# Layer 0 of a hybrid encoder: feature-major inputs from the host, and 1/rms applied behind the projections

## What is computed

```
h  = rms_norm(x, mix_norm_g)                 # x * rsqrt(mean(x^2) + eps) * g
proj = h @ w_in                              # 1024 x 4184 columns: mLSTM q,k,v,o and gates;
                                             # neighbourhood attention q,k,v; GLA q,k,v,g and a
x += mixer(proj) @ w_out                     # three kinds of heads, both directions
x += cross_attention(rms_norm(x, xattn_norm_g), rms_norm(mem, mem_norm_g))
x += (gelu(conv3(a)) * g) @ w_down           # a, g = rms_norm(x, ffn_norm_g) @ w_up
```

## Time and profile before

| | |
|---|---|
| median of 3 runs | 880.57 us (878.48 to 882.46) |
| time of the profiled execution | 878.24 us |
| its span, first to last instruction | 876.3 us |
| around the span | 1.9 us |
| TensorE busy | 861.8 us, 98% |
| VectorE busy | 596.0 us, 68% |
| ScalarE busy | 496.1 us, 57% |
| DMA | 146.78 MB, mean 168 GB/s |

### The profile page before, as it was taken

The page is one execution under the profiler, slowest core; times in us unless marked ns, Lnnn a source line. Parts: engine busy times, 40 slices in busy tenths (PEclk is TensorE's granted clock), DMA queues, the critical chain, the costliest instruction groups (busy, mean ns, idle before and its releaser), DMA issues.

```text
span 876.3 us, 14948 instructions
## 1 busy us (share of the span) xinstructions
PE 861.8 (98%) x6338; PEld 798.1 (91%) x6338; DVE 596.0 (68%) x820; ACT 496.1 (57%) x689; POOL 14.3 (2%) x35
## 2 busy tenths in 40 slices
PE   8999999999999999999999999999999899999997
PEld 8999998889889999999999999988898899999996
DVE  6887678757657666666577885887665666656655
ACT  7954663658647445445567546745755645445444
POOL 5000000000000000000000000000000000000000
PEclk9999999999999999999999999999999999999999
DMA  9735452364255555555448254335435365555541
GB/s 329 201 102 177 156 178 103 112 226 144 97 193 190 195 190 195 192 191 194 145 140 257 72 171 165 127 115 192 135 109 191 127 212 190 193 196 190 192 169 48
DMA packets 114665, 146.78 MB, mean 168 GB/s; under 512 B 10600, under 2 KB 94760, under 8 KB 114600
## 3 DMA queue, kind: packets, MB, share of 16 engines
q1 hardware_dynamic: 114456, 145.57, 49.7%
q10 hardware_dynamic: 144, 0.26, 0.1%
HBM read 144.77 MB, written 1.05 MB: 166 GB/s over the span
## 4 chain that ended last, share of the span: by engine, by line
PE 92%; ACT 3%; DVE 3%; issue 1%; DMA 0%; ACTq 0%; DVEq 0%
PE bank L665 26%; PE bank L666 25%; PE bank L667 25%; PE bank L706 4%; PE bank L743 2%; PE bank L832 2%; DVE wlo L1455 2%; PE bank L1017 2%; ACT whi L1096 1%; ACT yhi L1119 1%; PE bank L872 1%; PE bank L762 1%; PE bank L849 1%; DVE ylo L1710 1%; PE bank L882 1%
## 5 line engine op out<-in xcount | busy, mean ns | idle before, releaser
L1455 DVE TENSOR_TENSOR wlo<-raw,whi 128x2048 fp32r<-128x2048 f32 (+3 forms) x144 | 306.2, 2133 | 106.1 <-ACT whi L1096 105.2
L1096 ACT ACTIVATE whi<-raw 128x2048 fp32r<-128x2048 f32 (+3 forms) x144 | 257.4, 1793 | 53.5 <-PE bank L667 48.4
L665 PE MATMUL bank<-yhi,whi 128*128 128x256 f32 x704 | 195.1, 277 | 0.5 <-DVE ylo L1471 0.5
L666 PE MATMUL bank<-ylo,whi 128*128 128x256 f32 x704 | 194.6, 276 | 0.0
L667 PE MATMUL bank<-yhi,wlo 128*128 128x256 f32 x704 | 194.6, 276 | 0.0
L665 PEld LDWEIGHTS bank<-yhi,whi 128*128 128x128 f32 x704 | 132.2, 188 | 1.6 <-issue 0.7
L666 PEld LDWEIGHTS bank<-ylo,whi 128*128 128x128 f32 x704 | 132.2, 188 | 0.8
L667 PEld LDWEIGHTS bank<-yhi,wlo 128*128 128x128 f32 x704 | 132.2, 188 | 0.0
L665 PE MATMUL bank<-xhi,whi 128*128 128x256 f32 x320 | 91.4, 286 | 2.2 <-DVE wlo L1455 1.2
L665 PE MATMUL bank<-whi,xhi 128*128 128x512 f32 (+2 forms) x256 | 90.1, 352 | 0.0
L667 PE MATMUL bank<-xhi,wlo 128*128 128x256 f32 x320 | 88.9, 278 | 0.0
(11 more groups left out here) (268 smaller groups left out, 1373.1 us busy)
## 6 DMA issues: line engine op xcount, KB each, us to landing
raw<-in_w_up SPq DMA_DIRECT2D x44, 1024.0 KB, 5.0
raw<-in_w_down SPq DMA_DIRECT2D x22, 1024.0 KB, 4.8
raw<-in_w_in SPq DMA_DIRECT2D x10, 1024.0 KB, 7.3
raw<-in_w_xk SPq DMA_DIRECT2D x8, 1024.0 KB, 5.1
raw<-in_w_xv SPq DMA_DIRECT2D x8, 1024.0 KB, 4.9
raw<-in_w_out SPq DMA_DIRECT2D x8, 1024.0 KB, 4.8
raw<-in_w_xq SPq DMA_DIRECT2D x8, 1024.0 KB, 5.7
raw<-in_w_xo SPq DMA_DIRECT2D x8, 1024.0 KB, 4.9
```

The lines of the kernel that those rows point to most:

```text
L665: mm(o, s_hi, m_hi, start=first, stop=False, skip_group_check=True)
L666: mm(o, s_hi, m_lo, start=False, stop=False, skip_group_check=True)
L1096: A(weight(whi, gu), raw[:, gu % RING, 0:SIZE[gu]], ACT.Copy).then_inc(hi_done, 1)
L1455: tt(weight(wlo, gu), raw[:, gu % RING, 0:SIZE[gu]], weight(whi, gu), ALU.subtract).then_inc(lo_done, 1)
```

## The change

All of it is in layer 0, and the other layer keeps its code.

- The host passes x and mem a second time, laid out by features (`x_turned`, `mem_turned`, 1 MB each). The token-major x and mem are still loaded, x because it is the residual and gives the squares.
- xhi and xlo are made from the loaded blocks with the gain only. The two `normed`, the 16 transposes of x and the wait for x before gq go. gq, mix and qk0 are loaded and split in halves. nqk4 comes ahead of qk0. `keep_clock` runs 6 matmuls instead of 12.
- x itself is loaded after qk1. The squares follow the high part of qk1 on ScalarE; VectorE makes 1/rms as a column (`r1`, and half of it) and TensorE spreads it into a row on all partitions (`rx`, two matmuls in the midst of qk0), copied to `xr`.
- Feature-major results (mix, gq, nqk4, qk0 to qk2, nq, nk, gk) are multiplied by `xr` on VectorE. gq, nqk4, nq, nk and gk were emptied by ScalarE before. Token-major results (v, nv, gv, o, gg) get 1/rms as the scale of the ScalarE instruction that empties them already.
- mem: the squares are on ScalarE behind `conv(0)`, the row `rm` takes the place of the 16 transposes, and one VectorE instruction scales `memT` (128x2048) in head 3.
- GpSimd starts its constants at once, the parameter columns come in three DMAs, and half of qk1 is ahead of gp.

The diff, cut to its core:

```diff
+    if l:
+        fm("qk0", "w_in", (0, 256))
     fm("nqk4", "w_few", (2 * P, P))
+    if l == 0:
+        fm("qk0", "w_in", (0, 256))
     fm("qk1", "w_in", (256, 256))
...
+HALVED = ("gq", "mix", "qk0")
...
+        xr = carve(T)
...
+            def turned_rows(i):
+                sp.dma_start(xT[:, 2 * i:2 * i + 2, :], a["x_turned"][:, 2 * i:2 * i + 2, :]).then_inc(turned_in[i], 16)
             def load(gu):
                 if gu >= RING:
                     sp.wait_ge(lo_done, gu - RING + 1)
                 (l, _), m, k0, nk, cols = UNITS[gu]
                 dst = raw[:, gu % RING, 0:SIZE[gu]].rearrange("p (k n) -> p k n", k=nk)
+                if l == 0 and UNITS[gu][0][1] in HALVED:
+                    i = HALVED.index(UNITS[gu][0][1])
+                    c, n = cols[0]
+                    src = a[m][l, c // P] if m == "w_few" else a[m][l, :, c:c + n].rearrange("(k p) n -> p k n", p=P)
+                    sp.dma_start(dst[:, 0:4], src[:, 0:4]).then_inc(half_in[i], 16)
+                    if i == 0:
+                        turned_rows(0)
+                    sp.dma_start(dst[:, 4:KT], src[:, 4:KT]).then_inc(landed[gu % RING], 16)
+                    return
...
+                    for i in range(1, KT // 2):
+                        turned_rows(i)
+                if name == "qk2" and l == 0:
+                    for t in range(TT):
+                        sp.dma_start(h[:, t, :], a["x"][t * P:(t + 1) * P, :]).then_inc(tok_in[t], 16)
+                    sp.dma_start(pcols[:, 0, KT:], a["params"][:, 0, KT:]).then_inc(prm_in[0], 16)
                     sp.wait_ge(const_ready, 3)
                     load_gates(0)
+                if name == "va" and l == 0:
                     for t in range(TT):
                         sp.dma_start(mtm[:, t, :], a["mem"][t * P:(t + 1) * P, :]).then_inc(mem_in, 16)
+                if name == "vb" and l == 0:
+                    sp.dma_start(pcols[:, 1, :], a["params"][:, 1, :]).then_inc(prm_in[1], 16)
+                    sp.dma_start(memT[:], a["mem_turned"]).then_inc(mem_turned_in, 16)
...
-            pool.wait_ge(xn_ready, TT)
-            for v, x in ((gq, 0.0), (gk, 0.0), (perm, 0.0), (mlm, 0.0), (glm, 1.0), (bdm, 1.0), (win, 3e38),
-                         (ones, 1.0), (reset, 1.0), (mv, 1.0)):
+            for v, x in ((gq, 0.0), (gk, 0.0), (perm, 0.0), (ones, 1.0), (mv, 1.0)):
                 step(g.memset(v[:], x))
...
-            keep_clock(12, ps[BANK[0, "qk0"]])
+            keep_clock(6, ps[BANK[0, "qk0"]])
...
+                    fm_unit("nqk4", "n1")
+                else:
+                    fm_unit("nqk4", "n1")
+                    fm_blocks("qk0", "n1", [(0, 0, KT), (1, 0, 4)])
+                    pe.wait_ge(root_in, 1)
+                    free("rx")
+                    for t in range(TT):
+                        last = mm(bank("rx")[:, t * P:(t + 1) * P], r1[:, t, 0:1].broadcast_to([P, P]), ident[:], start=True, stop=True)
+                    last.then_inc(te_done, 1)
+                    fm_blocks("qk0", "n1", [(1, 4, KT)])
+                    fm_blocks("qk1", "n1", [(0, 0, 4)])
+                pe.wait_ge(const_ready, 4)
                 free("gp")
                 is_drained(pe, l, "mix")
                 mm(bank("gp")[0:64, 0:T], perm[:, 0, :], gsb[:, :], start=True, stop=True)
                 mm(bank("gp")[0:64, T:2 * T], perm[:, 1, :], gsb[:, :], start=True, stop=True).then_inc(te_done, 1)
-                if l:
-                    fm_blocks("qk1", "n1", [(0, 0, 4)])
+                fm_blocks("qk1", "n1", [(0, 0, 4) if l else (0, 4, KT)])
...
-                    pe.wait_ge(memn_ready, TT)
-                    for i in range(4):
-                        free(f"mt_{i}")
-                        for kk in range(2):
-                            for t in range(TT):
-                                k = 2 * i + kk
-                                last = nc.tensor.transpose(bank(f"mt_{i}", 2, T)[:, kk, t * P:(t + 1) * P],
-                                                           mtm[:, t, k * P:(k + 1) * P], ident[:])
-                        last.then_inc(te_done, 1)
+                    pe.wait_ge(mem_root_in, 1)
+                    free("rm")
+                    for t in range(TT):
+                        last = mm(bank("rm")[:, t * P:(t + 1) * P], rmem[:, t:t + 1].broadcast_to([P, P]), ident[:], start=True, stop=True)
+                    last.then_inc(te_done, 1)
...
+                def token_scale(t, half=0):
+                    return 0.5 ** half if l else r1[:, t, half:half + 1]
                 def take(nm):
+                    if l == 0 and nm in SCALED:
+                        return
...
+                def input_hi(ks):
+                    for k in ks:
+                        if k % 2 == 0:
+                            act.wait_ge(turned_in[k // 2], 16)
+                        A(xhi[:, k, :], xT[:, k, :], ACT.Copy, scale=pcol[:, R_MIX + k:R_MIX + k + 1]).then_inc(xhi_ready, 1)
                 if l == 0:
-                    act.wait_ge(prm_in, 16)
+                    hi_half("gq", 0)
+                    act.wait_ge(gain_in, 16)
+                    input_hi(range(2))
+                    hi_half("gq", 1)
+                    input_hi(range(2, KT))
+                    hi_half("mix", 0)
+                    hi_half("mix", 1)
+                    split_hi("nqk4")
+                    hi_half("qk0", 0)
+                    hi_half("qk0", 1)
+                    split_hi("qk1")
+                    for t in range(TT):
+                        act.wait_ge(tok_in[t], 16)
+                        square_all(h, t)
...
+                    act.wait_ge(prm_in[0], 16)
+                    act.wait_ge(const_ready, 4)
+                    act.wait_ge(mix_scaled, 1)
+                    b = mix_part
                 A(gsb[:, :], b[0:24, 0:T], ACT.Identity, bias=gbias[:, :])
                 A(gaT[96:128, :], b[96:128, 0:T], ACT.Copy)
                 A(gq[0:32, 1, :], b[32:64, 0:T], ACT.Copy, scale=32 ** -0.5)
                 drain(A(gk[0:32, 1, :], b[64:96, 0:T], ACT.Copy))
-                split_hi("qk1")
+                split_hi("qk1" if l else "qk2")
                 conv(0)
...
+                    act.wait_ge(mem_in, 16 * TT)
+                    for t in range(TT):
+                        square_all(mtm, t)
+                act.wait_ge(const_ready, 4)
...
+                    is_filled(act, l, "rm")
+                    drain(A(mr, bank("rm")[:, 0:T], ACT.Copy))
...
+                def input_lo(ks):
+                    for k in ks:
+                        hi_is(dve, l, "n1", k)
+                        stt(xlo[:, k, :], xT[:, k, :], pcol[:, R_MIX + k:R_MIX + k + 1], xhi[:, k, :], ALU.mult, ALU.subtract
+                            ).then_inc(xlo_ready, 1)
+                def xr_for(n):
+                    return xr.rearrange("p (o n) -> p o n", o=1).broadcast_to([P, n, T])
+                def scaled_qk(i):
+                    is_filled(dve, l, f"qk{i}")
+                    tt(qe[:, 2 * i:2 * i + 2, :], bank(f"qk{i}", 2, T), xr_for(2), ALU.mult).then_inc(scaled_ready, 1)
                 if l == 0:
+                    lo_half("gq", 0)
+                    input_lo(range(2))
+                    lo_half("gq", 1)
+                    input_lo(range(2, KT))
+                    lo_half("mix", 0)
+                    lo_half("mix", 1)
+                    split_lo("nqk4")
+                    lo_half("qk0", 0)
+                    lo_half("qk0", 1)
+                    split_lo("qk1")
                     for t in range(TT):
-                        dve.wait_ge(tok_in[t], 16)
-                        normed(t)
-                    dve.wait_ge(prm_in, 16)
-                    split_lo("gq")
-                turned("n1", R_MIX)
-                split_lo("nqk4")
-                if l == 0:
-                    dve.wait_ge(mem_in, 16 * TT)
-                    for t in range(TT):
-                        inverse_root(t)
-                        ts(mtm[:, t, :], mtm[:, t, :], rt[:, t:t + 1], None, ALU.mult).then_inc(memn_ready, 1)
-                split_lo("qk1")
+                        root_ready(t)
+                        link(V.reciprocal(r1[:, t, 0:1], rt[:, t:t + 1]))
+                    ts(r1[:, :, 1], r1[:, :, 0], 0.5, None, ALU.mult).then_inc(root_in, 1)
+                    is_filled(dve, l, "rx")
+                    drain(V.tensor_copy(xr, bank("rx")[:, 0:T]))
+                    is_drained(dve, l, "rx")
+                    is_filled(dve, l, "mix")
+                    tt(mix_part, bank("mix")[:, 0:T], xr, ALU.mult).then_inc(mix_scaled, 1)
+                    dve.wait_ge(const_ready, 4)
+                    is_filled(dve, l, "gq")
+                    drain(stt(gq[:, 0, :], bank("gq")[:, 0:T], 32 ** -0.5, xr, ALU.mult, ALU.mult))
+                    is_filled(dve, l, "nqk4")
+                    b = bank("nqk4")
```

(63 more changed lines are left out.)

138 lines of the change are left out of this document (86 added, 52 removed).

## The result

The changed kernel takes 887.9 us (median of 4 runs, 887.42 to 888.54) against 879.64 us (4 runs, 878.48 to 882.46) in the same session: ratio 1.0091, 95% interval 1.007 to 1.0111. It is slower by some 8 us; the prediction had said 881.7 with a range up to 886.0. The profiled execution took 888.38 us with a span of 886.4; the one of before took 878.24.

A forecast was written before the change was run, and what follows sets the result against it. VectorE was taken to bound nearly as much as TensorE at nq: of 5.5 us head start, waits of 4.85 left 0.6; heads cost 1.7, so +1.1 on 880.57 gave 881.7 us, range 876.0 to 886.0.

The forecast's parts named there:

- Everything behind is the same work with TensorE as its bound and keeps this shift.: After the heads of layer 0: all later work was to keep the shift of +1.1 us unchanged.
- the waits before the first head and nq: TensorE was to wait 2.95 us for `qk_ready` before the score product and 1.15 us for nq's low part.
- head start: TensorE's possible lead from an earlier mix and dropped memory transposes, less the added matmuls: 5.5 us if nothing else were late.
- The paragraph on the clock: At the start: with 12 warming passes the warming ends at 4.4 us, so gq may start at the lower clock.
- rival 4: The lower clock holds through gq into nqk4; 48 passes cost 5.6 us, 4.5 of it absorbed: 882.8 us, chance 0.10.
- qk1 at 14.85 (14.3 and 0.55): ScalarE takes qk1 at 14.85 us: DMA flow reaches its end at 14.3, plus 0.55 for the signal.
- root_in at 20.0: 1/rms of x ready for TensorE at 20.0 us, after squares, roots and reciprocals; TensorE waits 0.75 us.
- rival 3: Slower because x lands late: at 300 GB/s x comes 4.6 us later, giving 886.3 us; chance 0.16.
- With 1.4 us more (nq, nk): Head 2: VectorE's added nq and nk scaling delays the weights to 69.9 us, so TensorE waits 0.7.
- A wait of 1.0: Head 4: gv's second half has its low part at 85.5 us, wanted at 84.4; TensorE waits 1.0.
- Mix starts at 9.45.: Mix's first pass on TensorE was to start at 9.45 us instead of 14.10, a gain of 4.65 us.
- the slack of 0.4 us: In the kernel before, VectorE ends nq's low part at 51.01 us and TensorE starts nq at 51.42.

The follow-up runs named there:

- run 2: The changed kernel with dummy identity matmuls where TensorE waits: 13 before the first score product, 5 before nq, 7 before nv; 885.75 us, ratio 1.0065.
- run 12: The changed kernel with x loaded ahead of qk0, gk scaled before nv's low parts, and identity products in the waits before score product and nq; 881.35 us, ratio 1.0013.
- Run 5: Also called x_early: the changed kernel with token-major x issued ahead of qk0, its squares, roots and rx moved up too; 885.51 us, ratio 1.0074.
- Run 1: The changed kernel with gk scaled on VectorE ahead of the two low parts of nv; 885.77 us, ratio 1.0066.
- run 8: The kernel before with gk's bank emptied by VectorE behind the low part of nv's second half, not by ScalarE; 881.12 us, ratio 1.0017.
- Run 9: The kernel before with the memory's part alone: row rm for the 16 transposes, scaling in head 3; 878.43 us, ratio 0.9984.
- run 7: The changed kernel with 12 warming products of TensorE in front instead of 6; 890.1 us, one run.
- runs 10: The changed kernel with x ahead of qk0, gk scaled first, vb's low part on GpSimd and ScalarE's logarithm before vb's high part; 884.73 us, ratio 1.0053.
- 11: The kernel before with vb's low part made by GpSimd and ScalarE taking the logarithm first, as a control; 879.78 us, ratio 1.0002.

## Why the prediction was wrong

**The step that failed: "Everything behind is the same work with TensorE as its bound and keeps this shift."** The prediction priced a wait at its own length. It had the waits before the first head and nq almost exactly (2.95 and 1.15; they were 3.07 and 1.16), and took them for a head start used up. But TensorE came out of them at 1.2 GHz, and out of two more in head 2: 2.9 us at nq, 1.7 at nv, missing in the sum. This is the largest of its errors. The paragraph on the clock and rival 4 looked only at the warming. Runs 2 and 12 show it, the second against a number given beforehand (881.2 expected, 881.35 measured). The Trainium skill (TensorE: Matmul & The Clock Gate, "A second HAM failure mode") tells of a kernel whose TensorE was idle for short spells between groups of matmuls, so often that its clock was throttled again and again and the warming paid anew. The traces here agree in that waits of 1.2 to 3.1 us were followed by the lower level; they differ in that two of them were enough. The prediction had drawn on that page for the warming alone.

**"qk1 at 14.85 (14.3 and 0.55)" and "root_in at 20.0".** The queue was added up by bytes at 415 and 380 GB/s; qk1 lands at 17.13, 2.3 us late. Two things go against the sum. From 3 to 6 us the flow was 237 GB/s, 0.53 MB less than at 415 (1.3 us). And the sum left out the buffer: qk1 goes out only at 12.00, with mix's low part, and from 12.5 to 14 us the flow is 202 GB/s, 0.27 MB less than at 380 (0.7 us). No run separates the two. With qk1 the squares, root_in (22.26), `conv(1)` (38.15 for 35.3) and nq (53.89 for 50.8) are late. This is rival 3 at half its size. Run 5 took 2.4 us of the time back.

**"With 1.4 us more (nq, nk)" in head 2: a wait of 0.7.** It was 0.55 at that place, and 1.67 more that the step doesn't have: gk's scaling was added to VectorE's time, but what waits for it was not asked. It empties the bank that nv fills next, and VectorE does it behind 2.9 us of low parts. Run 1 took it away, and its trace has no low clock there; run 8 shows such a wait in the kernel before, at little more than its own price.

**"A wait of 1.0" at gv's second half** did not come: there is no wait at that place in the trace. Run 9 shows the memory's part as a gain of 1.0 to 1.4 us, where the prediction had let VectorE's 2.3 us eat most of the transposes.

**"Mix starts at 9.45."** It started at 12.31: the first 3 us of flow had 237 GB/s instead of 415, and gq ran at the low clock. For TensorE this cost next to nothing, as the prediction's own argument has it (ScalarE and VectorE set nq); run 7, with mix at 11.41 and no gain, agrees. But VectorE's low part of mix was as late (11.97 instead of some 10), and that is what held back qk1's buffer.

The sum with the measured terms: nq 2.5 late instead of 0.6 early, heads 6.9 instead of 1.7, 9.4 us in the profiled executions where 1.1 was forecast (10.1 measured between them, 8.3 between the medians). The 8.3 between 9.4 and 1.1 are 4.6 of clock, 3.1 from the later nq and 1.7 from gk's bank, less 1.1 for the waits that were shorter or did not come. Two slips in the working change little: the weights of head 2 come out at 70.1 by its own terms, not 69.9, and rival 3's x at 5.0 us of lateness, not 4.6. Right were the slack of 0.4 us as the point of the case, VectorE as what bounds nq, and no gain from the start. What stays open: some 1 us between run 12 and the kernel before, with 0.7 in two small waits in head 2; why the clock falls behind the pair of waits at nv in some executions and not in x_early's; and the price of the clock in most executions, since the medians of runs 1 and 2 fell by about half of what the stretch from nq to the last `mlo` shows.

## What to carry to other kernels

A head start on an engine that another one bounds is not merely lost: it becomes waits, and where TensorE waits twice or for long, it can come out at half its clock (here 2.9 us of loss behind 4.2 us of waits), so that the lead turns into a loss. When draining is moved from a free engine to one that works in order, ask for each bank who fills it next, and put the drain ahead of the work that nobody waits for yet. And reckon a queue by what frees its buffers as well as by its bytes.

## What the runs showed of the hardware

**Waits that lower the clock.** 3.07 + 1.16 us (the changed kernel) and 1.77 + 1.16 (x_early) were followed by some 6 us at the lower level. A single wait of 3.05 us was enough in run 1: the score product right behind it took 2.08 us instead of 1.13. The pair 0.55 + 1.67 was followed by some 3.5 us at the lower level in four traces and by none in x_early. A single 1.0 us (run 8) and 0.55 + 0.18 (run 1) were not. So the length of the waits alone does not decide it. Filling them with products of the identity kept 2.4 GHz in runs 2 and 12.

**Low clock without a cause in the edit.** Some executions lose 1.7 us elsewhere, once or twice: run 1 from 576 to 580 us, run 9 from 28 to 32, and run 8, which up to there is the kernel before, from 28 to 32 and again from 690 to 694:

```profile
28.00:30.00 2.00, 2.00 (x11) 0.66 0.94 258
30.00:32.00 2.00, 2.00 (x11) 0.50 0.84 191
```

Two of them would be a good part of the 3 to 4 us by which single runs of one kernel differ.

**GpSimd holds VectorE.** A tensor-tensor operation of VectorE with both inputs in SBUF took 3.54 us instead of 0.42 while GpSimd did one of its own, of some 3.7 us (runs 10 and 11). A scan that VectorE had begun before GpSimd's instruction took its usual 0.68. The Trainium skill (GPSIMD Engine Reference, 1. Specifications) names contention with VectorE instructions that have two SBUF inputs; the trace agrees.
